# First modulation columns fetched in four pairs, and the first tokens' products made pair by pair

## What is computed

```python
mod_l = (silu(c) @ w_ada + b_ada).reshape(9, 1024)        # for the latent tokens
mod_c = (silu(c_ctx) @ w_ada + b_ada).reshape(9, 1024)    # for the context tokens
h = x * (1 + scale) + shift            # shift = mod[0], scale = mod[1]
a = h @ w13                            # 1024 -> 2 * 2816
y = (silu(a[:, :2816]) * a[:, 2816:]) @ w2
x = layer_norm(ALPHA * x + 0.5 * gate * y)
```

## Time and profile before

| | us |
|---|---|
| median of 3 runs | 2441.8 |
| lowest and highest | 2439.67, 2447.35 |
| the profiled execution's own time | 2442.12 |
| its span | 2440.3 |
| TensorE busy in the span | 2291.9 |
| VectorE busy | 1389.5 |
| ScalarE busy | 803.3 |

### The profile page before, as it was taken

The page is one execution under the profiler, slowest core; times in us unless marked ns, Lnnn a source line. Parts: engine busy times, 40 slices in busy tenths (PEclk is TensorE's granted clock), DMA queues, the critical chain, the costliest instruction groups (busy, mean ns, idle before and its releaser), DMA issues.

```text
span 2440.3 us, 31857 instructions
## 1 busy us (share of the span) xinstructions
PE 2291.9 (94%) x12172; PEld 1963.7 (80%) x12186; DVE 1389.5 (57%) x2415; ACT 803.3 (33%) x1379; POOL 247.6 (10%) x204
## 2 busy tenths in 40 slices
PE   7999999999999999798899988979999999999996
PEld 6888888888788887697789877867878888877885
DVE  6676666666445365335642445754766565638735
ACT  2522222222243244422224324541533333323331
POOL 0000000000000010260000003520000000007303
PEclk9999999999999999899999999999999999999998
DMA  8153334344474454041000001031322223245442
GB/s 250 45 157 100 108 107 146 117 142 128 146 257 157 149 158 138 26 130 35 18 18 18 18 1 44 10 100 22 113 78 77 77 84 96 77 171 179 161 168 81
DMA packets 212188, 250.45 MB, mean 103 GB/s; under 512 B 13606, under 2 KB 161502, under 8 KB 212062
## 3 DMA queue, kind: packets, MB, share of 16 engines
q1 hardware_dynamic: 212062, 248.73, 33.0%
HBM read 208.05 MB, written 40.63 MB: 102 GB/s over the span
## 4 chain that ended last, share of the span: by engine, by line
PE 74%; DVE 12%; DMA 5%; ACT 5%; issue 2%; POOL 1%; SPq 1%; DVEq 0%; ACTq 0%; POOLq 0%
PE psum L1048 10%; PE psum L1049 10%; PE psum L1050 10%; PE psum L517 6%; PE psum L519 6%; PE psum L518 6%; DMA raw<-in_ffn_w 3%; PE psum L1497 2%; PE psum L1498 2%; PE psum L1499 2%; PE psum L1882 2%; PE psum L1068 1%; PE psum L1067 1%; PE psum L1066 1%; PE psum L1490 1%
## 5 line engine op out<-in xcount | busy, mean ns | idle before, releaser
L1048 PE MATMUL psum<-x_mix_h,x_op_h 128*128 128x512 f32 x640 | 249.9, 390 | 2.9 <-DVE v_sum L891 2.9
L1049 PE MATMUL psum<-x_mix_l,x_op_h 128*128 128x512 f32 x640 | 249.5, 390 | 0.0
L1050 PE MATMUL psum<-x_mix_h,x_op_l 128*128 128x512 f32 x640 | 249.0, 389 | 0.0
L801 ACT ACTIVATE x_op_h<-raw 128x512 fp32r<-128x512 f32 x140 | 86.0, 628 | 208.7 <-PE psum L1050 125.3
L801 ACT ACTIVATE x_op_h<-w_sum 128x512 fp32r<-128x512 f32 x160 | 97.5, 624 | 159.7 <-DVE w_sum L779 85.6
L1048 PEld LDWEIGHTS psum<-x_mix_h,x_op_h 128*128 128x128 f32 x640 | 120.3, 188 | 27.4 <-DVE x_op_l L807 3.4
L1050 PEld LDWEIGHTS psum<-x_mix_h,x_op_l 128*128 128x128 f32 x640 | 120.1, 188 | 25.2
L1049 PEld LDWEIGHTS psum<-x_mix_l,x_op_h 128*128 128x128 f32 x640 | 120.3, 188 | 23.3
L1143 POOL TENSOR_TENSOR ln_stats<-ln_stats,consts 128x1 f32<-128x1 f32 x26 | 17.0, 652 | 1198.1 <-DVE ln_stats L1138 1198.1
L807 DVE TENSOR_TENSOR x_op_l<-raw,x_op_h 128x512 fp32r<-128x512 f32 x140 | 92.8, 686 | 44.4 <-ACT x_op_h L801 42.1
L1497 PE MATMUL psum<-p_wh,xh_lat 128*128 128x256 f32 x384 | 111.5, 290 | 0.0
(11 more groups left out here) (373 smaller groups left out, 6101.7 us busy)
## 6 DMA issues: line engine op xcount, KB each, us to landing
raw<-in_ffn_w SPq DMA_DIRECT2D x198, 512.0 KB, 4.9
ada_slice<-in_w_ada SPq DMA_DIRECT2D x56, 512.0 KB, 3.9
f_rows<-g_out SPq DMA_DIRECT2D x88, 256.0 KB, 2.3
p_raw<-in_w_in SPq DMA_DIRECT2D x22, 512.0 KB, 4.8
g_raw_a<-f_rows SPq DMA_DIRECT2D x44, 256.0 KB, 3.8
ada_early<-in_w_ada SPq DMA_DIRECT2D x16, 512.0 KB, 5.4
y<-in_x SPq DMA_DIRECT2D x16, 512.0 KB, 9.4
x_rows<-y SPq DMA_DIRECT2D x16, 512.0 KB, 3.4
```

The source lines that it names most:

```text
L801: nc.scalar.activation(op_tiles(F, op)[0][:], OP_SOURCE[op], ACT.Copy).then_inc(F.hi, 1)
L1048: nc.tensor.matmul(o, wh[:, k], high(k), start=i < 4 and k == 0, stop=False, skip_group_check=i > 3)
L1049: nc.tensor.matmul(o, wh[:, k], low(k), start=False, stop=False, skip_group_check=i > 3)
L1050: last = nc.tensor.matmul(o, wl[:, k], high(k), start=False, stop=k == KH - 1, skip_group_check=i > 3)
```

## The change

The 16 pieces become eight of 256 columns (1 MB, rows of 1 KB): shift 0, scale 0, shift 1, scale 1 and so on; pair m covers units 2m and 2m+1 of the turn. Four token tiles and the first weight block are fetched ahead of them, the second weight block after the second pair, the other token tiles last. TensorE multiplies the four scale pieces and the last shift piece; VectorE makes the sums of the first three shift pieces. As soon as a pair is known, its two units are scaled and split, and their products with weight block 0 are made (`first_steps`), behind the next pair's columns. The items of the first layer are reordered: block 0 chunk 0, block 1 chunk 0, block 0 chunk 1, block 0 context, block 1 chunk 1, block 1 context. Chunk 1 is transposed in item 1 and the context in item 2. In the second layer nothing changes but that its lists are written out.

Cut to its core:

```diff
-        ada_early = place("ada_early", 0, [P, ADA_EARLY, KD, P])
-        early_sum = place("early_sum", 144, [P, ADA_EARLY, 2, P])
+        early_at = (96, 32, 48, 64)
+        early_shift = [place(f"early_shift{m}", at, [P, KD, 2 * P]) for m, at in enumerate(early_at)]
+        early_scale = [place(f"early_scale{m}", at + 8, [P, KD, 2 * P]) for m, at in enumerate(early_at)]
...
+                self.items = [(0, 0), (1, 0), (0, 1), (0, 2), (1, 1), (1, 2)] if self.n == 3 else [(0, 0), (0, 1), (1, 0), (1, 1)]
...
+        def first_sp(sp):
+            for t in range(4):
+                sp.dma_start(y[:, t, :], token_rows(t)).then_inc(x_in[0], 16)
             for i in range(2):
-                w13_piece(sp, F, i, 0)
+                w13_piece(sp, F1, i, 0)
+            early_loads(sp)
+            for t in range(4, TA):
+                if t == 4:
+                    sp.wait_ge(early_used, 2)
+                sp.dma_start(y[:, t, :], token_rows(t)).then_inc(x_in[t // 4], 16)
+            for i in range(2):
+                sp.wait_ge(F1.lo, i + 3)
+                w13_piece(sp, F1, i, 2)
+            for i in range(6):
+                plain_stored(sp, F1, i)
...
+        def early_loads(sp):
+            for i in range(2 * EARLY):
+                m, piece = i // 2, (early_shift, early_scale)[i % 2][i // 2]
+                if i >= 3:
+                    sp.wait_ge(early_in[i % 3], 16 * (i // 3))
+                at = D * (i % 2) + 2 * P * m
+                sp.dma_start(piece[:], ada_view[:, :, at:at + 2 * P]).then_inc(early_in[i % 3], 16)
+                if i == 3:
+                    for part in range(2):
+                        sp.wait_ge(F1.lo, part + 1)
+                        w13_piece(sp, F1, part, 1)
+        def early_pe(pe, m, i=1):
+            piece = (early_shift, early_scale)[i][m]
+            wait_early(pe, 2 * m + i)
+            for n in (2 * m, 2 * m + 1):
...
+                for k in range(KD):
+                    last = nc.tensor.matmul(psum[:, 7, at:at + 2], piece[:, k, cols], more_c[:, k, :],
                                             start=k == 0, stop=k == KD - 1)
+            last.then_inc(early_used, 1)
+        def early_known_dve(dve, m):
+            dve.wait_ge(early_used, 2 * m + 2)
+            for to, at, bias in ((in_scale, 0, early_bias[:, 0]), (in_shift, 2 * KD, early_bias[:, 1])):
+                last = nc.vector.tensor_tensor(...)
+            last.then_inc(mod_ready, 1)
...
+        def first_pe(pe, rows_wait):
+            turned = lambda k: turn_pe(pe, T1, T1_BANKS, rows_wait, (0, k))
+            for m in range(EARLY):
+                turned(2 * m)
+                turned(2 * m + 1)
+                if m == EARLY - 1:
+                    early_pe(pe, m, 0)
+                early_pe(pe, m)
+                if m:
+                    first_steps(pe, m - 1)
+                if m < EARLY - 1:
+                    early_shift_pe(pe, m)
+            first_steps(pe, EARLY - 1)
+        def first_steps(pe, m):
+            if m == 0:
+                pe.wait_ge(F1.lo, 2)
+            for k in (2 * m, 2 * m + 1):
+                pe.wait_ge(T1.low, k + 1)
+                for part in range(2):
+                    last = plain_step(pe, F1, 0, part, k)
+            if m == EARLY - 1:
+                last.then_inc(F1.ab_ready, 1)
...
-            scale_known(act)
-            half_act(act, F1, T1, T1_BANKS, 0, range(KD))
             first_high(act, F1)
+            for m in range(EARLY):
+                act.wait_ge(mod_ready, m + 1)
+                half_act(act, F1, T1, T1_BANKS, 0, (2 * m, 2 * m + 1))
+                if m == 1:
+                    second_block_high(act, F1)
+            silu(act, F1, 0)
             half_act(act, F1, T1, T1_BANKS, 1, range(KD))
-            second_block_high(act, F1)
-            silu(act, F1, 0)
+            silu(act, F1, 1)
             turn_act(act, T1, T1_BANKS, turn_buf1, lambda a: None, 2)
...
             first_low(dve, F1)
+            for m in range(EARLY):
+                if m < EARLY - 1:
+                    early_sums_dve(dve, m)
+                if m:
+                    half_dve(dve, F1, T1, 0, (2 * m - 2, 2 * m - 1))
+                early_known_dve(dve, m)
+                if m == 2:
+                    second_block_low(dve, F1)
+            half_dve(dve, F1, T1, 0, (KD - 2, KD - 1))
+            glu(dve, F1, 0)
             half_dve(dve, F1, T1, 1, range(KD))
-            second_block_low(dve, F1)
-            glu(dve, F1, 0)
+            glu(dve, F1, 1)
             turn_dve(dve, T1, turn_buf1, 2)
-            glu(dve, F1, 1)
             for k in range(KH):
                 mix_sums(dve, F1, T1, k)
                 mix_low(dve, F1, X1.mix_order[2 * k:2 * k + 2])
                 if k == 1:
                     glu(dve, F1, 2)
+            glu(dve, F1, 3)
             mix_low(dve, F1, X1.mix_order[8:12])
-            glu(dve, F1, 3)
...
+            plain_pe(pe, F1, 1, T1, lambda part, k: turn1(1, (KD * part + k) // 2) if k % 2 else None)
+            plain_pe(pe, F1, 2, T1, lambda part, k: turn1(2, (KD * part + k) // 2) if k % 2 else None)
+            for i in range(3, 6):
+                plain_pe(pe, F1, i, T1)
```

More of the change, by code:

```diff
@@ L560, in piece_sums, with wait_early, early_sums_dve @@
+        def wait_early(engine, i):
+            engine.wait_ge(early_in[i % 3], 16 * (i // 3 + 1))
+        def early_sums_dve(dve, m):
+            wait_early(dve, 2 * m)
+            for k in range(KD):
                 for v in range(2):
[L561 removed]
+                    n = 2 * KD * m + 2 * k + v
+                    factor, sums = more[:, v * KD + k:v * KD + k + 1], early_sum[:, m, v]
                     if k:
[L563 to L567 removed]
@@ L569, in early_pe @@
[L569 to L573, removed]
-                pe.wait_ge(early_in[n % 3], 16 * (n // 3 + 1))
+                        dve.wait_ge(early_dve, n - 1)
+                        nc.vector.scalar_tensor_tensor(sums, early_shift[m][:, k], factor, sums, op0=ALU.mult, op1=ALU.add)\
+                            .then_inc(early_dve, 1)
+                    else:
+                        nc.vector.tensor_scalar_mul(sums, early_shift[m][:, k], factor).then_inc(early_dve, 1)
@@ new lines, in early_shift_pe @@
+        def early_shift_pe(pe, m):
+            pe.wait_ge(early_dve, 2 * KD * (m + 1))
+            for n in (2 * m, 2 * m + 1):
+                cols = slice((n % 2) * P, (n % 2 + 1) * P)
+                for v in range(2):
+                    at = 2 * KD + 2 * n + v
+                    last = nc.tensor.matmul(psum[:, 7, at:at + 1], early_sum[:, m, v, cols], ones[:], start=True, stop=True)
+            last.then_inc(early_used, 1)
+        def early_known_dve(dve, m):
+            dve.wait_ge(early_used, 2 * m + 2)
+            for to, at, bias in ((in_scale, 0, early_bias[:, 0]), (in_shift, 2 * KD, early_bias[:, 1])):
+                last = nc.vector.tensor_tensor(to[:, :, 2 * m:2 * m + 2],
+                                               psum[:, 7, at + 4 * m:at + 4 * m + 4].rearrange("p (a b) -> p b a", b=2),
+                                               bias[:, 2 * m:2 * m + 2].unsqueeze(1).to_broadcast([P, 2, 2]), ALU.add)
+            last.then_inc(mod_ready, 1)
@@ new lines, in plain_step @@
+        def plain_step(pe, F, i, part, k):
+            b, n = F.items[i]
+            at, size = F.chunks[n]
+            o = psum[:, 2 * (i % 2) + part, 0:size]
+            wh, wl = F.w_high(b, part)[:, k], F.w_low(b, part)[:, k]
+            high, low = F.X.part(0, k, at, size), F.X.part(1, k, at, size)
+            nc.tensor.matmul(o, wh, high, start=k == 0, stop=False)
+            nc.tensor.matmul(o, wh, low, start=False, stop=False)
+            return nc.tensor.matmul(o, wl, high, start=False, stop=k == KD - 1)
@@ new lines, in plain_pe @@
+        def plain_pe(pe, F, i, turn, beside=lambda part, k: None):
+            b, n = F.items[i]
+            pe.wait_ge(F.lo, 2 * b + 2)
+            if i >= 2:
+                pe.wait_ge(F.glu_ready, i - 1)
+            for part in range(2):
+                for k in range(KD):
+                    if b == 0 and part == 0:
+                        pe.wait_ge(turn.low, KD * n + k + 1)
+                    last = plain_step(pe, F, i, part, k)
+                    beside(part, k)
+            last.then_inc(F.ab_ready, 1)
@@ L2803, in gates3 @@
                 gate_rows_pe(pe, N3, 8, 0, 6)
-            plain_pe(pe, F2, T3, lambda n, k: turn_pe(pe, T3, T3_BANKS, norm2_done, (n, k)))
+            pe.wait_ge(T3.scaled, KD)
+            plain_pe(pe, F2, 0, T3, lambda part, k: turn_pe(pe, T3, T3_BANKS, norm2_done, (1, k)) if part else None)
+            for i in range(1, 4):
+                plain_pe(pe, F2, i, T3)
             quick2_pe(pe, lambda: gates3(pe))
```

118 lines of the change are left out of this document (33 added, 85 removed).

## The result

The median went from 2443.69 us (2439.67 to 2447.73) to 2465.63 us (2454.02 to 2469.27), over eight runs each: ratio 1.0086, 95% interval 1.0068 to 1.0104. That is slower by 21.9 us, where I had forecast no change.

A forecast was written before the change was run, and what follows sets the result against it. VectorE was taken to bound the plain stage: 2.7 us delay at the first quick product, less 0.9 recovered, net +1.8 on 2442.1, giving 2443.9, or 2443.6 on the median basis: no change within 0.3%; range 2433 to 2452 us.

The forecast's parts named there:

- Part 3: Opening, pair by pair: priced chain of columns, sums, low parts and products, with item 0 ending at 65.6 us.
- Part 1: Transfer order in the opening: 3.0 us per piece, shift 0 in at 17.4, last modulation piece at 42.0 us.
- Part 2: Opening loop: VectorE's sums, 6.1 us per pair, set the rhythm.
- Part 4: From item 0 to quick stage: VectorE bounds it, first quick product at 125.0 us, 2.7 later than before.
- my two signs of being wrong: Quick stage starting before 118 us, or TensorE not standing before item 4.
- The recovered 0.9 us: Wait behind the second operand load, early quick stage: load follows 0.9 us sooner, leaving net +1.8 us.
- The slow clock: Rival, opening bursts: each runs wholly at 1.2 GHz, item 0 +5.7 us, time 2449.3 us; chance 0.2.
- The fall to 0.50: Granted clock at 192.70 to 196.00 us in the profile before, after 32 small products; cited for the slow clock.
- VectorE's queue does not hold TensorE: Rival, stretch before the quick stage: TensorE's 6.3 us gain would stay, time 2435.5 us; chance 0.13.
- The overlap doesn't come about: Rival, opening: item 0 does not start before the last piece and ends at 71.8, time 2449.8 us; chance 0.05.

The follow-up runs named there:

- e1_half_small: Changed kernel with half of the contraction of the modulation columns left out, so half the small products; median +6.0 us against the kernel before, ratio 1.0027.
- e4_reorder_alone: Kernel before with the new item order alone, its opening untouched; median +5.1 us against the kernel before, ratio 1.0027.
- e2_gate_first: Changed kernel with item 2's gating ahead of the mixed sums on ScalarE and VectorE; median +18.8 us against the kernel before, ratio 1.0083.
- e3_mix_between: Changed kernel with two rounds of mixed sums between the context's units, item 2's gating right after; median +12.7 us against the kernel before, ratio 1.0063.
- e6_dense_before: Changed kernel with twelve 512-column products into an unused bank ahead of the first two-column products; single run, first quick product at 139.9 us.
- e5_shift3_vector: Changed kernel with the last shift piece summed on VectorE like the other three; median +14.4 us against the kernel before, ratio 1.0063.
- e10_units_first: e9_before_item0_early with the first three units transposed before TensorE waits for the weights; median -2.0 us against the kernel before, ratio 0.9982.
- e9_before_item0_early: Kernel before, pieces unchanged, with first weight block fetched and split earlier and item 0 multiplied as units are turned; median -5.4 us, ratio 0.9982.

## Why the prediction was wrong

**The step that failed** is the first line of prices in Part 3: "a pair's 16 two-column products 3.5", and beside it "four one-column products 0.9". These count the products of the code at the price of a record of the trace. Measured: 32 records and 6.6 to 7.0 us for a piece, 8 records and 1.84 us for pair 0's one-column products (0.95 to 1.07 for those behind a burst). The rows shown could have said so: the 16 records at 33.63 are one piece of 128 columns, eight products in the code.

Item 0's last product came at 84.9 in place of 65.6, 19.3 us late. Laid against the steps of Part 3, the transfers make 1.0 of this, the four stretches of small products between the bursts 15.6 (3.3, 3.2, 2.2 and 6.9), and the three bursts 2.7. With the count set to mine (e1_half_small) 14.5 of the 15.6 went. That is less than the 5 x 3.5 = 17.5 us by which the five pieces were mispriced, since in pairs 1 and 2 a part would have stood under VectorE's sums and low parts anyway.

- **Part 1, transfers: right.** The tokens were in at 11.9 (10.8), shift 0 at 18.40 (17.4) and scale 0 at 21.44 (20.4): about 1 us late all along, and 3.0 us from one piece to the next, as taken. That is 345 GB/s for 1.05 MB, between the 296 of the 512-byte rows and the 407 of the 4 KB rows; the transfer engines read nine tenths busy or more in both openings. So the rule of the Trainium skill ("DMA: Bandwidth & Descriptors", Specifications) that 512 bytes already give full rate did not hold for these reads.
- **Part 2: the sums right, their role wrong.** A pair's sums run from 18.40 to 24.56, 6.16 us for the 6.1 worked out. They did not set the rhythm: with columns of 7 us in the loop, TensorE did. With half of them (e1_half_small) VectorE did, as forecast.
- **Part 3: wrong**, as above. The overlap itself came about: the first real product is at 39.54, in place of 59.31 before and of the 32 forecast.
- **Part 4: right, step by step**, only from a later start. Mixed sums 29.7 us after item 0's end (30.2 worked out), TensorE's wait before item 4 6.1 (6.6), 13 slow products after it (eight), first quick product 59.3 after item 0's end (59.4). e4_reorder_alone shows the same 58.8 on the kernel before, and e2_gate_first and e3_mix_between show that it is VectorE's list that counts. What it means is harder than I put it: with 58.8 us from item 0's silu to the quick stage, the change could only have gained with that silu before 63.5. Neither of my two signs of being wrong showed, since both were about this part; what did show it was the first large product, at 39.54.
- **The recovered 0.9 us: wrong.** The wait behind the second operand load grew from 1.7 to 3.0 us. In SP's timelines the first load of that stage is issued 2.4 us after the first quick product in both kernels (124.70 and 146.60): it stands behind the stores of item 5, whose gating also follows that product by 1.0 both times. The load then took longer to land (6.4 against 5.6 us median in the page's part on DMA issues for that stretch). Why it did was not tried.
- **The rivals.** The slow clock was real but small: the first burst ran wholly at 0.43 us a start, the second nine of its 12, the closing one some 14 of 24. It is 2.7 of the 19.3 us above, and the two levels show in the window 61.0 to 84.9 with a granted clock of 0.57. The fall to 0.50 speaks less for this rival than I wrote: there TensorE had 32 one-column products without a gap ahead of it, not a wait. The waits in the changed kernel do bear it out (0.50 behind the 6.1 us). "VectorE's queue does not hold TensorE" is refuted. "The overlap doesn't come about" did not happen. None of them was about TensorE's own load in the opening, and the range ended at 2452 because every bound in it was about rates, none about a count.

## What to carry to other kernels

Before a price per record of a trace is multiplied by a count from the code, count one group both ways: here 64 products in the code were 128 records, and the error stood in five pieces on the chain that set the time. When work is split so that a stage can begin early, write down for each engine what one round of the loop costs it, the small products too: the overlap brought the first real product 20 us forward, and still the item ended 9 us later. And of two engines that meet at a later point, only the one that comes last repays an edit: taking away a 6 us wait of TensorE gave nothing, while work put into VectorE's gaps brought the quick stage 4.7 us nearer to item 0.

## What the runs showed of the hardware that I had not expected

- **Records.** A float32 product with two columns or one leaves two records, while a 128x128 transpose leaves one (32 for eight units of four), and so does a product of split operands (64 of L698 with the latent tokens for 64 in the code). A product of one or two columns costs 0.42 to 0.43 us at the lower clock (6.69 us for 16 of two columns in the changed kernel, 6.82 for 16 of one column in the one before) and 0.22 at the higher (3.58 for 16, e6_dense_before): one column costs what two do.
- **The clock.** TensorE was nearly always busy between 28.3 and 54.6 us in the changed kernel, yet a burst of 12 large products once ran wholly at the lower level (39.54 to 44.80) with the small ones behind it fast (eight records in 1.07 us), and in the next the clock rose after nine. The small products followed the level that they found and did not hold it: 32 records took 3.72 us behind dense work (e6_dense_before), 4.59 in e5_shift3_vector, and 6.5 to 7.0 in the changed kernel. Kernels with the same opening ended item 0 anywhere from 80.9 to 85.1 us (after, e2_gate_first, e3_mix_between). In e10_units_first the first large product, 1.3 us after transposes without a break, ran at the higher level at once; in e9_before_item0_early, with 3.3 us of idle time ahead of the transposes, six ran slow. I can't say from these runs what decides it.
- **A lead that doesn't last.** Median and first quick product moved together within 3 us in most kernels, but e4_reorder_alone paid 4.8 us less than its trace says and e10_units_first gained 5.3 less. The stages behind, whose instructions are the same, differ by up to 8 us from trace to trace (1770.7 and 1778.2 in the two above). From the first quick product on, e9_before_item0_early took 2296.5 us to that last `w2` product, e10_units_first 2307.1 and the kernel before 2301.0. Large products at the lower clock (0.60 us or more each in the timelines) explain only a part: there are 60, 78 and 83 of them, at some 0.2 us lost each. Followed by the same instructions of VectorE, e10_units_first leads the kernel before by 6.3 us until 1448 us, by 1.4 at 1599 and by 0.8 at 2196, so most is lost in some steps inside the token mixer; in one of them eight small products took 1.65 us in place of 1.13. What sets these steps off stays open; so a gain of this size in the opening is only known from repeated runs.
